# Three MLPs: one up product of 512 columns for both halves of the activations

## The reference

```
def squared_relu_mlp(h, w1, w2):          # m1, layer 2 of the first block
    return jnp.square(jax.nn.relu(h @ w1)) @ w2
def sq_relu_mlp(h, w_in, w_out):          # m2, m3, the second block
    a = jax.nn.relu(h @ w_in)
    return (a * a) @ w_out
# h: 256 x 1024, w1: 1024 x 4096, w2: 4096 x 1024, all float32
```

## Time and profile before

| | |
|---|---|
| median of 3 runs | 1312.89 us (1311.13 to 1314.19) |
| profiled execution | 1313.38 us, span 1311.6 us from first to last instruction |
| granted TensorE clock over the span | 0.991 |
| PE / PEld / DVE / ACT / POOL busy | 96% / 83% / 66% / 53% / 10% of the span |
| m1, m2, m3 on TensorE | about 180, 189 and 179 us of the span |

### The profile page before, as it was taken

One profiled execution on the slowest core, in us unless ns is written; L12 is line 12 of the kernel. 1 busy time (PEld: TensorE's weight loads), 2 busy tenths in 40 slices (PEclk: granted clock), 3 DMA queues, 4 the chain that ended last, 5 costly groups with the idle time before them and its releaser, 6 DMA issues.

```text
span 1311.6 us, 21556 instructions
## 1 busy us (share of the span) xinstructions
PE 1258.9 (96%) x8320; PEld 1092.7 (83%) x8320; DVE 860.6 (66%) x1501; ACT 691.9 (53%) x1219; POOL 136.9 (10%) x154
## 2 busy tenths in 40 slices
PE   6899999999999999999999989999999999999999
PEld 4798799889799656889898867889998778899997
DVE  6578699898675675786546774665565566654444
ACT  3466454445455665644445874644444565654542
POOL 1012121121100000100100320100100100010100
PEclk7899999999999999999999999999999999999999
DMA  9879569999489151585653522686554554466650
GB/s 365 327 261 324 182 217 372 359 339 371 156 243 293 49 177 65 181 315 185 190 170 109 177 94 79 153 324 181 174 179 142 176 177 138 153 183 200 180 160 32
DMA packets 123780, 267.37 MB, mean 204 GB/s; under 512 B 11040, under 2 KB 33824, under 8 KB 123296
## 3 DMA queue, kind: packets, MB, share of 16 engines
q1 hardware_dynamic: 119328, 257.23, 59.1%
q0 software_dynamic: 1728, 6.29, 1.5%
q10 hardware_dynamic: 2624, 2.49, 0.6%
HBM read 264.83 MB, written 1.15 MB: 203 GB/s over the span
## 4 chain that ended last, share of the span: by engine, by line
PE 63%; DVE 5%; ACT 3%; issue 1%; POOL 1%; DVEq 0%; ACTq 0%; POOLq 0%
PE bank L538 12%; PE bank L540 11%; PE bank L539 11%; PE ps_s L538 3%; PE ps_s L539 3%; PE ps_s L540 3%; PE ps_p L538 3%; PE ps_p L539 3%; PE ps_p L540 3%; PE ps_s L1324 1%; DVE wlo L1619 1%; PE ps_p L1167 1%; PE ps_p L1143 1%; POOL rs L3444 1%; PE ps_s L1131 1%
## 5 line engine op out<-in xcount | busy, mean ns | idle before, releaser
L1619 DVE TENSOR_TENSOR wlo<-wring,whi 128x1024 fp32r<-128x1024 f32 (+1 forms) x376 | 457.9, 1228 | 262.5 <-ACT whi L2765 258.3
L2765 ACT ACTIVATE whi<-wring 128x1024 fp32r<-128x1024 f32 (+1 forms) x376 | 388.2, 1045 | 359.2 <-PE bank L540 135.1
L538 PE MATMUL bank<-h_hi,whi 128*128 128x256 f32 (+1 forms) x1224 | 348.7, 285 | 4.9 <-DVE wlo L1619 1.8
L539 PE MATMUL bank<-h_lo,whi 128*128 128x256 f32 (+1 forms) x1224 | 346.2, 283 | 0.0
L540 PE MATMUL bank<-h_hi,wlo 128*128 128x256 f32 (+1 forms) x1224 | 346.2, 283 | 0.0
L538 PEld LDWEIGHTS bank<-h_hi,whi 128*128 128x128 f32 (+1 forms) x1224 | 233.9, 191 | 10.7 <-issue 8.9
L539 PEld LDWEIGHTS bank<-h_lo,whi 128*128 128x128 f32 (+1 forms) x1224 | 234.0, 191 | 0.8
L540 PEld LDWEIGHTS bank<-h_hi,wlo 128*128 128x128 f32 (+1 forms) x1224 | 234.0, 191 | 0.0
L3460 POOL TENSOR_TENSOR ex<-ex 128x512 f32<-128x512 f32 x64 | 81.6, 1278 | 666.5 <-ACT g_hi L2896 666.5
L538 PE MATMUL bank<-whi,h_hi 128*128 128x512 f32 (+2 forms) x232 | 93.5, 403 | 12.8 <-DVE wlo L1619 10.4
L538 PE MATMUL ps_s<-whi,g_hi 128*128 128x512 f32 x256 | 101.0, 394 | 0.6 <-DVE wlo L1619 0.6
(11 more groups left out here) (391 smaller groups left out, 1763.5 us busy)
## 6 DMA issues: line engine op xcount, KB each, us to landing
wring<-in_mlp_w SPq DMA_DIRECT2D x128, 512.0 KB, 5.2
wring<-in_mlp_w_in SPq DMA_DIRECT2D x64, 512.0 KB, 3.9
wring<-in_mlp_w_out SPq DMA_DIRECT2D x64, 512.0 KB, 4.0
wring<-in_ada_w_t SPq DMA_DIRECT2D x48, 512.0 KB, 8.0
wring<-in_ada_w SPq DMA_DIRECT2D x36, 512.0 KB, 6.3
wring<-in_moba_w_qkv SPq DMA_DIRECT2D x24, 512.0 KB, 3.9
wring<-in_a_qk SPq DMA_DIRECT2D x16, 512.0 KB, 7.2
wring<-in_kv_ada_w_t SPq DMA_DIRECT2D x16, 512.0 KB, 6.9
```

The source lines that it names most:

```text
L538: nc.tensor.matmul(out, lh, rh, start=first, stop=False, skip_group_check=mixed)
L539: nc.tensor.matmul(out, lh, rl, start=False, stop=False, skip_group_check=mixed)
L1619: v.tensor_tensor(piece_view(wlo, p), raw_view(p), piece_view(whi, p).bitcast(F32), ALU.subtract).then_inc(lo_ready, 1)
L2765: a.activation(piece_view(whi, p), raw_view(p), ACT.Copy).then_inc(hi_ready, 1)
```

## The change

In m1, m2 and m3 (`JOINED`) the up product is done by `by_halves`. `h_hi` and `h_lo` become the two halves of one tile `h_both`. For each n and k one matmul with the weight's high half moves 512 columns, the high and low activations side by side, into a whole bank; a second one with the weight's low half adds 256 columns to the bank's right half. The sum of left and right half is the product. So each chunk has 32 matmuls of 512 and 32 of 256 columns in place of 96 of 256, and takes four banks in place of two; all four are waited for before its first matmul.

Behind it ScalarE copies the right half of each bank to a buffer `rest`, VectorE adds it to the left half and writes `hidden` (`join`, at the step after the last up piece), and ScalarE takes relu in place and the square from there. The two g_low come one step later than before. In m2 the lookup moves into the middle of down(c-1), ahead of its third piece, and VectorE empties its bank at j % 8 = 3 rather than 5.

```
--- before.py
+++ after.py
@@ -221,8 +221,8 @@
 
         wring = sb("wring", [P, SLOTS, PIECE])
         x_res = sb("x_res", [P, TT, D])
-        h_hi = sb("h_hi", [P, KT, T], F32R)
-        h_lo = sb("h_lo", [P, KT, T], F32R)
+        h_both = sb("h_both", [P, 2, KT, T], F32R)
+        h_hi, h_lo = h_both[:, 0, :, :], h_both[:, 1, :, :]
         whi = sb("whi", [P, PIECES, PIECE], F32R)
         wlo = sb("wlo", [P, PIECES, PIECE], F32R)
 
@@ -280,6 +280,8 @@
         gl = sb("gl", [P, KT])
         LAZY = ["l", "m2", "o", "m3"]
         FAST = ["m0", "kv", "m1"]
+        JOINED = ["m1", "m2", "m3"]
+        rest = att[:, 0:D].rearrange("p (i t) -> p i t", t=T)
         x_sums = {"l": stat[:, 18:20], "m2": stat[:, 20:22], "m3": stat[:, 22:24]}
         lazy_eps = {"l": stat[:, 24:26], "o": stat[:, 26:28]}
         o_root = stat[:, 28:30]
@@ -575,6 +577,28 @@
                 for g in range(2):
                     piece_of[key + (g,)] = p
 
+            def by_halves(key, ready=None):
+
+                banks = [bank_take(pe, key + (n,)) for n in range(4)]
+                for j in range(KT // 2):
+                    p = piece_wait()
+                    wh, wl = piece_view(whi, p), piece_view(wlo, p)
+                    for n in range(4):
+                        out = bank[:, banks[n], :]
+                        for k in (2 * j, 2 * j + 1):
+                            if ready and n == 0:
+                                ready(k)
+                            at = (slice(None), k % 2, slice(n * P, (n + 1) * P))
+                            nc.tensor.matmul(out, wh[at], h_both[:, :, k, :], start=(k == 0), stop=False,
+                                             skip_group_check=True)
+                            last = nc.tensor.matmul(out[:, T:2 * T], wl[at], h_hi[:, k, :], start=False,
+                                                    stop=(k == KT - 1), skip_group_check=True)
+                        if n < 3 and j == KT // 2 - 1:
+                            last.then_inc(filled[banks[n]], 1)
+                    piece_over(last, key + (3,) if j == KT // 2 - 1 else None)
+                for n in range(4):
+                    piece_of[key + (n,)] = p
+
             def by_token(key, src, kt, readers=1, first_k=0, between=None, apart=False, step=None):
 
 
@@ -759,6 +783,9 @@
                 y = [ps_s[:, 0, :], ps_s[:, 1, :], ps_p[:, 0, :], ps_p[:, 1, :]]
 
                 def up(c):
+                    if tag in JOINED:
+                        by_halves((f"{tag}_w1", c), (lambda k: wait(tag, k)) if c == 0 else None)
+                        return
                     by_pairs((f"{tag}_w1", c), (h_hi, h_lo), (lambda k: wait(tag, k)) if c == 0 else None)
 
                 def down_part(c, k, p, t, n):
@@ -768,10 +795,12 @@
                     return product(y[2 * t + n], (g_hi[g], g_lo[g]), (wh[:, 0, cols], wl[:, 0, cols]),
                                    c == 0 and k == 0, c == 7 and k == 3)
 
-                def down(c):
+                def down(c, middle=None):
                     pe.wait_ge(sem("mlp_glo"), 16 * int(tag[1]) + 2 * c + 2)
                     if c < 7:
                         for k in range(4):
+                            if middle and k == 2:
+                                middle()
                             p = piece_wait()
                             for t in range(TT):
                                 for n in range(2):
@@ -795,9 +824,7 @@
                 up(0)
                 for c in range(1, 8):
                     up(c)
-                    if beside and c >= 2:
-                        beside(c - 2)
-                    down(c - 1)
+                    down(c - 1, (lambda: beside(c - 2)) if beside and c >= 2 else None)
                 if before_last:
                     before_last()
                 down(7)
@@ -1863,7 +1890,18 @@
             def mlp(tag, ada=(), other=None, last=None, first=0):
                 ada = list(ada)
                 base = first_piece[(f"{tag}_w1", 0)]
-                due = {}
+                due, joins = {}, {}
+
+                def join(c):
+
+                    for n in range(4):
+                        i, key = 4 * c + n, (f"{tag}_w1", c, n)
+                        if n % 2 == 0 and 2 * c + n // 2 >= 3:
+                            dve.wait_ge(sem("mlp_glo"), 16 * int(tag[1]) + 2 * c + n // 2 - 2)
+                        dve.wait_ge(sem("mlp_rest"), 32 * JOINED.index(tag) + i + 1)
+                        src = bank_full(dve, key)
+                        v.tensor_tensor(hidden[:, (2 * c + n // 2) % 3, (n % 2) * T:(n % 2 + 1) * T], src[:, 0:T],
+                                        rest[:, i % 4, :], ALU.add).then_inc(drained[uses[key][0]], 1)
 
                 def g_low(b):
 
@@ -1875,11 +1913,16 @@
 
                 for j in range(64):
                     p = base + j
+                    if j in joins:
+                        join(joins[j])
                     if j in due:
                         g_low(due[j])
                     key = pieces[p][0]
                     if key[0].endswith("w1") and p == first_piece[key] + 3:
-                        due.update({j + 1: 2 * key[1], j + 2: 2 * key[1] + 1})
+                        behind = 2 if tag in JOINED else 1
+                        due.update({j + behind: 2 * key[1], j + behind + 1: 2 * key[1] + 1})
+                        if tag in JOINED:
+                            joins[j + 1] = key[1]
                     if first <= j < first + 4 * len(ada):
                         n = j - first
                         matvec(ada[n // 4], n % 4)
@@ -2445,7 +2488,7 @@
                     v.tensor_tensor(onehot[s % 2], nearest, spread[s], ALU.is_equal).then_inc(
                         sem("onehot_ready"), 1)
                     dve.wait_ge(sem("onehot_ready"), s + 1)
-                if j % 8 == 5 and 0 <= j // 8 - 2 < LOOKUPS:
+                if j % 8 == 3 and 0 <= j // 8 - 2 < LOOKUPS:
                     s = j // 8 - 2
                     src = bank_full(dve, ("bias2", s)).rearrange("p (m k h) -> p k h m", k=4, h=8)
                     to = bias2.rearrange("p h (k c) -> p k h c", k=4)[:, :, :, 16 * s:16 * s + 16]
@@ -2881,8 +2924,35 @@
                         if u >= 1:
                             copy(u - 1)
 
+            def joined_mlp(tag):
+
+                if tag in x_sums:
+                    act.wait_ge(sem("x_squared"), 2 * list(x_sums).index(tag) + 2)
+                for c in range(8):
+                    for n in range(4):
+                        i, key = 4 * c + n, (f"{tag}_w1", c, n)
+                        src = bank_full(act, key)
+                        if c:
+                            bank_emptied(act, (f"{tag}_w1", c - 1, n))
+                        a.activation(rest[:, i % 4, :], src[:, T:2 * T], ACT.Copy).then_inc(sem("mlp_rest"), 1)
+                    for half in range(2):
+                        b = 2 * c + half
+                        for n in (2 * half, 2 * half + 1):
+                            bank_emptied(act, (f"{tag}_w1", c, n))
+                        h = hidden[:, b % 3, :]
+                        a.activation(h, h, ACT.Relu).then_inc(sem("mlp_relu"), 1)
+                        if c >= 2:
+                            act.wait_ge(*read_end[first_piece[(f"{tag}_w2", c - 2)] + 3])
+                        act.wait_ge(sem("mlp_relu"), 16 * JOINED.index(tag) + b + 1)
+                        a.activation(g_hi[:, c % 2, 2 * half:2 * half + 2, :], h.rearrange("p (i t) -> p i t", t=T),
+                                     ACT.Square).then_inc(sem("mlp_ghi"), 1)
+                keep_ahead("act", first_piece[(f"{tag}_w2", 7)])
+
             def mlp(tag):
 
+                if tag in JOINED:
+                    joined_mlp(tag)
+                    return
                 for b in range(2 * FF // W):
                     key = (f"{tag}_w1", b // 2, b % 2)
                     src = bank_full(act, key)
```

## The result

The changed kernel takes **1320.1 us** (median of 4 runs, 1318.98 to 1320.83) against 1313.47 us for the kernel before in the same session, a ratio of 1.004 with a 95% interval of 1.0024 to 1.0056. It is slower by about 5 us by the ratio (the two medians are 6.6 us apart). A second session gave 1318.68 (median of 12 runs) against 1314.75, a ratio of 1.0029 (1.0015 to 1.0043). The forecast was 1311.1 us, range 1307.0 to 1317.5. All ratios here compare runs in the same, fast state; three single runs far above the rest (2469.95 us of the kernel before, 2064.60 of e7_bias_early, 1777.23 of e11_equal) are left out of them.

What follows compares the result with a forecast made beforehand. The prediction took TensorE's list of matmuls to bound the kernel. Its terms, -10.1 + 4.35 + 4.0 = -1.75 us, gave 1311.1 us, with a range of 1307.0 to 1317.5.

Steps and rivals of the forecast that it cites:

- What bounds the kernel: Over the three MLPs, TensorE is almost always busy, so time is the number of matmuls times their distance, plus any waits.
- Step 1: Up products of m1, m2, m3: two matmuls in place of three gain 13.1 ns each, 10.1 us over 768.
- the operand of two runs: Wide matmul's moving operand, 256 high and 256 low columns apart: cost bounded at 0 and 13.1 ns, taken as 0.
- The 2.5 ns of the Trainium skill: The skill's fixed part of a warm matmul: the change would gain only 1.9 us, time about 1319.
- Step 2: up(1) waits for VectorE to join the last of up(0)'s four banks: 1.45 us per MLP, 4.35 us lost.
- E: The moment at which TensorE's next matmul could start after up(0); the last join was forecast to end at E + 1.25.
- Step 3: In m2, up chunks 3 to 7 wait for the bias add to empty the lookup's bank: 0.8 us each, 4.0 lost.
- The first rival: Waits smaller than computed: the bias add comes before the chunk needs it, 1307.1 us, or 1309.1 with half; chance 0.20.
- The second (VectorE's backlog decides): In m2, a 1.1 us delay of VectorE's path makes each of five waits 1.0 us longer: 1316.1 us; chance 0.20.
- At nothing: ScalarE's copies and VectorE's adds, about 1.5 us per chunk on each, lie beside TensorE; the moved lookup costs TensorE the same.
- the wide matmul keeps the fixed cost: If a two-run operand costs 13.1 ns, the matmul gain is gone and 8.35 us of waits stay: 1321.2 us; chance 0.08.

Runs made afterwards that it cites:

- e7_bias_early: The changed kernel with VectorE emptying the lookup's bank at j % 8 = 2, ahead of the two lookup operands, not at 3: 1314.74 us, ratio 0.9994.
- e11_equal: The changed kernel with both matmuls of an up product 384 columns wide, activation halves adjacent, part of the product left out: 1315.87 us, ratio 1.0.
- e4_three: The changed kernel with the wide matmul split into two of 256 columns; four banks, joins and moved lookup kept: 1324.82 us, ratio 1.0077.
- e1_adjacent: The changed kernel with high and low activations adjacent for each k, so the wide operand is one run of 512: 1319.41 us, ratio 1.0043.
- e3_both: The changed kernel with adjacent activation halves and each bank waited for just ahead of its first matmul: 1311.74 us, ratio 0.998.
- e8_pairs_late: The changed kernel with two wide matmuls, then two narrow ones, and each bank waited for just ahead of its first matmul: 1308.6 us, ratio 0.9951.
- e6_grouped: The changed kernel with eight wide, then eight narrow matmuls in a chunk's first three pieces, pairs in the last, banks taken late: 1307.66 us, ratio 0.9936.

## Why the prediction was wrong

**What bounds the kernel: right.** TensorE's list and its waits account for the result in every kernel of the table.

**Step 1 failed, as a size.** The fixed cost per matmul is real: three matmuls a product cost some 5 us more than two (e4_three). But the forecast gain of 10.1 us, 13.1 ns a product, came out at 7.2 ns (360.0 - 352.8), 0.23 us a chunk. Down chunks behind it are slightly longer (10.94 against 10.91 us), so a pair of chunks went from 22.42 to 22.23, and 24 times 0.19 is 4.6 us. The same 4.6 is left when the waits are taken off the stages' +3.86 (3.86 - 4.5 - 4.0). The step failed where it added distances from the earlier trace rows, each read in a stream of equal matmuls, and laid them on a stream in which two widths alternate. There 353 ns a product is the rate of every chunk entered without a wait; the forecast rate was reached in six chunks of 24, all behind a wait, and they are in these net sums with about 1.2 us. The prediction bounded the operand of two runs, which costs nothing (e1_adjacent), and left out the order. It did say that it would be wrong if the distances behind a wide matmul differed; it gave this neither a price nor a chance. Equal widths have their fixed 13 to 14 ns in e11_equal as in the earlier trace rows (11.12 us / 64 less 160 ns), so the fixed part itself was read rightly. What in TensorE makes the alternating stream slower stays open. The 2.5 ns of the Trainium skill ("TensorE: Matmul & The Clock Gate", section "Wait — 56ns, not 53.3ns?") would have given a time nearer to the measured one (about 1319, by the prediction's estimate), but that would have been luck: these streams contradict its reason.

**Step 2: right.** Forecast 1.45 us three times, 4.35 in all; measured 4.5 with the restart, and 1.41 each (4.2) by the stages of e4_three. VectorE's own queue was the later path, as computed. The last join ended at E + 1.20 in m1 (E is 543.42 + 0.12, forecast 1.25), and TensorE followed 0.25 us later rather than 0.14.

**Step 3: right.** Forecast 0.8 us five times, 4.0 in all; measured 4.0 net in the profiled execution and 3.7 in the second. The mechanism is as described, but that the number fits so well is in part luck: waits and restarts alone are 4.6 us, 0.9 each, and two chunks at the faster rate bring the net down to 4.0. The prediction's own terms gave 0.74, which it rounded up to 0.8. The first rival (smaller waits) is out. The second (VectorE's backlog decides) came as near as was computed: the high split is ready at 958.63, and VectorE is free at 958.73, and the low split that needs both starts at 958.76; the extra 1.0 us per wait of that rival did not come.

**At nothing: right but for 0.3 us.** VectorE's 24 us and ScalarE's 31 us of added work lie beside TensorE; with the waits removed (e3_both) the stages are shorter than before, with the same added work. The moved lookup was not quite free: in e4_three, where nothing else of the down chunks changed, those of m2 take 82.40 us from start to start, waits left out, against 82.07.

**The sum.** -10.1 + 4.35 + 4.0 = -1.75 was forecast. Measured are -4.6 + 4.5 + 4.0 = +3.9 over the MLPs. Nearly all of the 5.6 us between the two lies in step 1. The rival with the right sign and nearly the right time (1321.2, the wide matmul keeps the fixed cost) had the wrong cause and 0.08. With a price for alternation, even one bounded from 0 to 13.1 ns, the range would have had to reach above 1320.

## What to carry to other kernels

A distance between matmuls holds for the stream it was read in, and one chunk need not stand for all: look at those behind a wait as well. Where an edit makes widths alternate, bound the price of the order by itself, and put equal widths side by side where dependences allow; here pairs were enough. Where a chunk takes several banks, wait for each just ahead of its first use, and let the engine that empties a bank do so before the side work that can wait: the two waits that ate the gain here cost 8.5 us, and two small edits on TensorE's side (e8_pairs_late, e6_grouped) turn a change that loses 0.3 to 0.4% into one that wins 0.5 to 0.6%.

## What had not been expected of the hardware

- A matmul of 512 columns and one of 256 in strict alternation take 353 ns in every chunk entered without a wait, and 353 or 347 behind one; in pairs they take 348, in groups of eight 349, and two of 384 columns 347. Neither the operand's layout, nor the bank, nor the weight tile changes the first number. What in TensorE makes it so stays open.
- A down chunk of equal matmuls is 0.03 us longer behind an up chunk at the slower rate (10.94 against 10.91); behind up(1) of m3, which ran at the faster one, it is 10.91, and e11_equal shows 10.92.
- The lower clock level stands for 3.41 us at one place in some executions and not in others, at 529.4 us in one of two profiles of the same program; between m1 and m2 such a stretch costs about 1.5 us.
